# Cached attention of a hybrid decoder step in two sets of four sequences, with the value pages behind the delta rule

## The reference, cut to what matters

```python
kmean = mean of each 256-key block                 # 4 blocks, 8 heads, 8 sequences
gate  = q . kmean ; keep the 3 best past blocks    # per head and sequence
s = q . k * hd ** -0.5 over the kept blocks and the own key
p = softmax(s) ; o = p @ v                         # float32
```

## Time and profile before

| | us |
|---|---|
| median of three runs | 596.73 (593.17 to 600.68) |
| the profiled execution's own time | 596.88 |
| its span | 594.9 |
| TensorE busy | 534.4 (90%) |
| VectorE busy | 350.0 (59%) |
| ScalarE busy | 163.5 (27%) |
| mean granted clock of TensorE | 0.947 |

### The profile page before, as it was taken

One profiled execution on the slowest core, in us unless ns is written; L12 is line 12 of the kernel. 1 busy time (PEld: TensorE's weight loads), 2 busy tenths in 40 slices (PEclk: granted clock), 3 DMA queues, 4 the chain that ended last, 5 costly groups with the idle time before them and its releaser, 6 DMA issues.

```text
span 594.9 us, 10233 instructions
## 1 busy us (share of the span) xinstructions
PE 534.4 (90%) x3943; PEld 450.2 (76%) x3943; DVE 350.0 (59%) x548; ACT 163.5 (27%) x230; POOL 56.6 (10%) x126
## 2 busy tenths in 40 slices
PE   7879997997998888988789689987999999999997
PEld 5557775675688766865564059887999999999996
DVE  4540269478798787955734537465665566455441
ACT  4101010811132122211000224364343443424420
POOL 6800010000104800000101000000000000000000
PEclk8979897997699999999969899998999999999999
DMA  9996356476049467643739998595465655645201
GB/s 294 332 302 207 108 189 218 123 204 221 19 150 324 144 221 245 217 132 119 244 111 376 384 352 268 173 298 163 148 209 162 195 169 168 195 144 193 73 19 37
DMA packets 98998, 116.79 MB, mean 196 GB/s; under 512 B 6317, under 2 KB 81278, under 8 KB 98934
## 3 DMA queue, kind: packets, MB, share of 16 engines
q1 hardware_dynamic: 93218, 104.42, 54.8%
q10 hardware_dynamic: 3908, 7.42, 3.5%
q0 software_dynamic: 1824, 4.30, 2.6%
HBM read 113.30 MB, written 2.99 MB: 195 GB/s over the span
## 4 chain that ended last, share of the span: by engine, by line
PE 64%; DVE 21%; DMA 7%; ACT 3%; issue 3%; ACTq 1%; SPq 0%; DVEq 0%
PE bank L336 61%; DVE prod L916 5%; DVE s_all L1019 5%; DVE mats L916 3%; DMA ring<-in_ada_w_dram 2%; DMA ring<-in_w_out_dram 2%; DVE BTP L916 1%; DVE cv L1127 1%; DMA ring<-in_cache_v_dram 1%; DMA x_nat<-in_x_sample_dram 1%; PE bank L373 1%; PE bank L382 1%; ACT w_part L1692 1%; DMA qb<-q_rows_dram 1%; PE bank L517 1%
## 5 line engine op out<-in xcount | busy, mean ns | idle before, releaser
L336 PE MATMUL bank<-a_hi,w_part 128*128 128x264 f32 x832 | 153.5, 286 | 2.1 <-DVE a_lo L1464 2.1
L916 DVE TENSOR_TENSOR w_part<-ring,w_part 128x2048 fp32r<-128x2048 f32 (+1 forms) x38 | 84.9, 2236 | 89.2 <-ACT w_part L1692 89.2
L336 PEld LDWEIGHTS bank<-a_hi,w_part 128*128 128x128 f32 x832 | 129.8, 189 | 2.6 <-issue 2.6
L336 PE MATMUL bank<-a_lo,w_part 128*128 128x264 f32 x416 | 118.4, 285 | 0.0
L1692 ACT ACTIVATE w_part<-ring 128x2048 fp32r<-128x2048 f32 (+1 forms) x38 | 70.9, 1871 | 86.0 <-PE bank L336 75.0
L336 PE MATMUL bank<-hT,ring 128*128 128x264 f32 x352 | 85.7, 406 | 0.8 <-ACT proj L1555 0.8
L336 PEld LDWEIGHTS bank<-hT,ring 128*128 128x128 f32 x352 | 70.0, 201 | 14.9 <-issue 2.4
L336 PEld LDWEIGHTS bank<-a_lo,w_part 128*128 128x128 f32 x416 | 79.0, 190 | 0.1
L336 PE MATMUL bank<-hid_hi,w_part 128*128 128x264 f32 x352 | 64.9, 285 | 0.0
L336 PEld LDWEIGHTS bank<-ident 128*128 128x128 f32 x362 | 48.1, 212 | 10.4 <-issue 5.6
L336 PEld LDWEIGHTS bank<-hid_hi,w_part 128*128 128x128 f32 x352 | 54.5, 188 | 0.1
(11 more groups left out here) (326 smaller groups left out, 570.3 us busy)
## 6 DMA issues: line engine op xcount, KB each, us to landing
ring<-in_ada_w_dram SPq DMA_DIRECT2D x24, 1024.0 KB, 7.3
ring<-in_cache_k_dram SPq DMA_DIRECT2D x64, 256.0 KB, 3.6
ring<-in_w_in_dram SPq DMA_DIRECT2D x11, 1024.0 KB, 5.6
ring<-in_w_gate_dram SPq DMA_DIRECT2D x11, 1024.0 KB, 5.3
ring<-in_w_up_dram SPq DMA_DIRECT2D x11, 1024.0 KB, 5.3
ring<-in_cache_v_dram SPq DMA_DIRECT2D x40, 256.0 KB, 4.2
ring<-in_w_down_dram SPq DMA_DIRECT2D x8, 1024.0 KB, 5.1
ring<-in_cache_v_dram ACTq DMA_DIRECT2D x24, 256.0 KB, 5.2
```

Source lines behind the costliest of these rows:

```text
L336: return pe.matmul(out, lhsT, rhs, start=start, stop=stop, skip_group_check=True)
L916: return v.tensor_tensor(out, a, b_, op)
```

## The change

The eight sequences are split into two sets of four (`GS`, `GW`). Each set has its own block sums (`G0`, `G1`), maxima, denominators, probabilities and fold (`FO0`, `FO1`), at half the width. Set 0's chain stands between the heads of the prompt attention, and its pages follow the delta rule's end (`V0` to `V3`); the last key item, `K15`, and set 1's `G1` stand among them. `DMAX1` and `DEXP1` follow, with `A9` and `XA` between, then `V4` to `V7` between `XB` and `XD`. `OWN` keeps only the own key's score and moves to before `L1`.

A set's pages now add up in one bank: each sequence has its own 8 of 32 stationary columns, and there is no masking or folding per sequence. At a set's end ScalarE copies the bank (`pv_rows`) and eight matmuls with `selq` select each head's columns and turn them at once. Set 0's probabilities lie in the upper half of `prod`, so the key items of sequences 4 to 7 use the lower half, in four instructions of 1024 columns (`k_item_low`). GpSimd clears the two halves in turn, and stores the tails ahead of the pooling. All pages are issued by SP. `K0` comes after `W8`, and the idle matmuls ahead of the heads' turns are distributed anew. (`QB` tokens have no part on any engine; they are dropped.) The last operations of `OWN` in the old list are the first of `G`.

```diff
+    GS = NS // 2
+    GW = GS * NPG * H
...
-    ORDER = ("W1 W2 QSUM W7 QNORM QR QB0 QB1 K0 W8 K1 K2 W9 CEXT W10 CONV BA AB W3 DSUM QB2 K3 W4 DNORM KSUM K4 GN W5 "
-             "QB3 K5 GC KNORM GBC KR ROWS KK W6 K6 QB4 TI VR L1 K7 KROW W0 K8 M1 VROW L2 QB5 K9 M2 TAILS L3 S K10 M3 A4 "
-             "H0 QB6 K11 L4 M4 H1 A5 H2 L5 K12 M5 A6 QB7 H3 K13 H4 L6 K14 M6 POOL H5 UA A7 K15 H6 UB UC H7 UD A8 HE OWN "
-             "A9 DMAX DEXP V0 XA V1 XB V2 XC V3 XD V4 MX V5 V6 MW0 V7 VE MD MW1").split()
+    ORDER = ("W1 W2 QSUM W7 QNORM QR W8 K0 K1 W9 K2 CEXT W10 CONV BA AB W3 DSUM K3 W4 DNORM KSUM K4 GN W5 "
+             "K5 GC KNORM GBC KR ROWS KK W6 K6 TI VR OWN L1 K7 KROW W0 K8 M1 VROW L2 K9 M2 TAILS L3 S K10 M3 A4 H0 L4 "
+             "H1 M4 A5 K11 H2 L5 M5 H3 G0 A6 H4 L6 DMAX0 K12 M6 POOL H5 DEXP0 UA K13 H6 UB A7 UC H7 K14 UD A8 V0 HE K15 "
+             "V1 G1 V2 V3 FO0 DMAX1 A9 XA DEXP1 V4 XB V5 XC V6 XD MX MW0 V7 FO1 MD MW1").split()
...
-        selc = tmp("selc", [P, NS, 32])
-        dm8 = tmp("dm8", [P, H])
+        selq = tmp("selq", [P, H, GS])
...
-        cmp4 = prod[:, 1024:1024 + NS * NB * H].rearrange("p (q n h) -> p q n h", q=NS, n=NB)
-        pP = prod[:, :].rearrange("p (a m) -> p a m", m=32)
+        pP = [prod[:, o:o + 1024].rearrange("p (a m) -> p a m", m=32) for o in (1024, 0)]
...
+        cmp4 = [w_b[:, o:o + GS * NB * H].rearrange("p (q n h) -> p q n h", q=GS, n=NB) for o in (GW, 0)]
...
-                for _ in range((14, 8, 2, 16, 4, 4, 18, 6)[h]):
+                for _ in range((14, 4, 14, 4, 6, 6, 10, 10)[h]):
...
             def own_scores():
-                keep_awake(6, 8)
                 pe.wait_ge(sem("own_diag"), 1)
-                b = opened("own", 6)
+                b = opened("own", 3)
...
+            def group_sums(g):
+                if g:
+                    keep_awake(6, 8)
+                pe.wait_ge(sem("k_scored"), GS * (g + 1))
+                b = opened(f"gsT{g}", (3, 6)[g])
+                mm(b[:, 0:GW], ones[:, :], s_all[:, g * GW:(g + 1) * GW])
+                for n in range(2):
+                    o = g * GW + n * P
+                    last = pe.transpose(b[:, GW + n * P:GW + (n + 1) * P], s_all[:, o:o + P], ident[:, :])
+                closed(last, f"gsT{g}")
...
+            def spread_max(g):
+                    keep_awake(5, 9)
+                pe.wait_ge(sem("max_diag"), g + 1)
+                b = opened(f"pmax{g}", (3, 5)[g])
+                closed(mm(b[:, 0:GW], ones[:, :], w_a[:, g * GW:(g + 1) * GW]), f"pmax{g}")
...
+            def denominators(g):
+                    keep_awake(5, 5)
+                pe.wait_ge(sem("exps"), g + 1)
+                b = opened(f"den{g}", (3, 6)[g])
+                closed(mm(b[:, 0:GW], ones[:, :], w_b[:, g * GW:(g + 1) * GW]), f"den{g}")
...
             def page_values(q):
-                if q == 0:
-                    keep_awake(4, 9)
-                    pe.wait_ge(sem("p_ready"), 1)
-                b = opened(f"pv{q}", 4 + q % 2)
+                g, j = q // GS, q % GS
+                if j == 0:
+                    if g:
+                        keep_awake(4, 6)
+                    pe.wait_ge(sem("p_ready"), g + 1)
+                    opened(f"pv{g}", (3, 4)[g])
+                b = bank[(3, 4)[g]]
                 for hf in range(HALVES):
                     slot = arrived(pe, ("v", (q, hf))).rearrange("p (k n) -> p k n", k=PGI)
                     for k in range(PGI):
-                        last = mm(b[32 * k:32 * k + 32, :], pP[:, q * NPG + hf * PGI + k, :], slot[:, k, :],
-                                  hf == 0, hf == HALVES - 1)
-                    if hf < HALVES - 1:
+                        last = mm(b[32 * k:32 * k + 32, :], pP[g][:, j * NPG + hf * PGI + k, :], slot[:, k, :],
+                                  j + hf == 0, j == GS - 1 and hf == HALVES - 1)
+                    if j < GS - 1 or hf < HALVES - 1:
                         used_up(last, ("v", (q, hf)), "pe_read")
-                closed(last, f"pv{q}")
-                read_by(f"pv{q}", ("v", (q, HALVES - 1)))
-                if q:
-                    fold(q - 1)
-            def page_end():
-                keep_awake(4, 8)
-                closed(fold(NS - 1), "y8")
-                keep_awake(5, 4)
-                pe.wait_ge(sem("y8_out"), 1)
-                b = opened("yT8", 7)
+                if j == GS - 1:
+                    closed(last, f"pv{g}")
+                    read_by(f"pv{g}", ("v", (q, HALVES - 1)))
+            def fold(g):
+                if g:
+                    keep_awake(5, 6)
+                pe.wait_ge(sem("pv_rows"), g + 1)
+                b = opened(f"yT{g}", (3, 7)[g])
                 for c in range(AC):
-                    last = pe.transpose(b[:, c * P:(c + 1) * P], w_a[:, c * P:(c + 1) * P], ident[:, :])
-                closed(last, "yT8")
+                    for h2 in range(2):
+                        r = 64 * h2
+                        last = mm(b[r:r + 64, c * GS:(c + 1) * GS], stg[:, g, c * P + r:c * P + r + 64], selq[:, 2 * c + h2, :])
+                closed(last, f"yT{g}")
...
+            def k_item_low(q, hf):
+                item = ("k", (q, hf))
+                slot = arrived(v, item)
+                v.wait_ge(sem(f"qb{q % 2}"), 16 * (q // 2 + 1))
+                half = PGI // 2
+                for w in range(2):
+                    ins = tt(prod[:, 0:1024].rearrange("p (k n) -> p k n", k=half),
+                             slot[:, 1024 * w:1024 * w + 1024].rearrange("p (k n) -> p k n", k=half),
+                             bc(qb[:, q % 2:q % 2 + 1, :], [P, half, AW]), ALU.mult)
+                    if w:
+                        used_up(ins, item, "keys_read")
+                        v.wait_ge(*released[item])
+                    else:
+                        step(ins)
+                    o = (q * NPG + hf * PGI + w * half) * H
+                    ins = v.tensor_reduce(s_all[:, o:o + half * H], prod[:, 0:1024].rearrange("p (g d) -> p g d", d=HD),
+                                          AX, ALU.add)
+                    if w and hf == HALVES - 1:
+                        ins.then_inc(sem("k_scored"), 1)
+                        v.wait_ge(sem("k_scored"), q + 1)
+                    else:
+                        step(ins)
...
+            def group_gates(g):
+                v.wait_ge(sem("tails_out"), 64)
+                gate, cnt, cmp = of(gate4, g), of(cnt4, g), cmp4[g]
+                b = full(v, f"gsT{g}")
+                v.tensor_reduce(flat(gate4, g), b[:, 0:GW].rearrange("p (n t h) -> p n h t", t=PPB, h=H), AX, ALU.add)
+                freed(v.tensor_reduce(tokmax[:, 2 * g:2 * g + 2], b[:, GW:2 * GW].rearrange("p (n t) -> p n t", n=2), AX, ALU.max),
+                      f"gsT{g}")
+                v.wait_ge(bank_free[filled[f"gsT{g}"][0]], frees_at(f"gsT{g}"))
+                for n in range(2):
+                    o = g * GW + n * P
+                    last = v.tensor_scalar(w_a[:, o:o + P], ident[:, :], tokmax[:, 2 * g + n:2 * g + n + 1], None, ALU.mult)
+                inc(last, "max_diag")
+                step(v.memset(cnt, 0.0))
                 for m in range(NB):
                     for n0, n1, op in ((0, m + 1, ALU.is_gt), (m + 1, NB, ALU.is_ge)):
                         if n0 < n1:
...
+                            last = tt(cmp[:, :, n0:n1, :], bc(gate[:, :, m:m + 1, :], [P, GS, n1 - n0, H]),
+                                      gate[:, :, n0:n1, :], op)
                     step(last)
...
+                    step(tt(cnt, cnt, cmp, ALU.add))
+                step(v.tensor_scalar(flat(gate4, g), flat(cnt4, g), float(min(TOPK, NB + 1)), None, ALU.is_lt))
+                step(v.tensor_scalar(flat(cnt4, g), flat(gate4, g), FAR, -FAR, ALU.mult, ALU.add))
+            def spread_max(g):
+                e = w_b[:, g * GW:(g + 1) * GW]
+                sm0, sm1, sm2, sm3 = (sm64[:, n, g * GS:(g + 1) * GS, :] for n in range(4))
+                b = full(v, f"pmax{g}")
+                freed(tt(paged(e), paged(b[:, 0:GW]), bc(flat(cnt4, g).unsqueeze(2), [P, GS * NB, PPB, H]), ALU.add), f"pmax{g}")
+                v.wait_ge(bank_free[filled[f"pmax{g}"][0]], frees_at(f"pmax{g}"))
+                step(v.tensor_reduce(sm0, queried(e).rearrange("p q n h -> p q h n"), AX, ALU.max))
+                step(tt(sm1, sm0, sm2, ALU.max))
+                tt(sm3, sm2, sm1, ALU.subtract)
+                step(tt(queried(e), queried(s_all[:, g * GW:(g + 1) * GW]), bc(sm1.unsqueeze(2), [P, GS, NPG, H]), ALU.subtract))
+                inc(v.tensor_scalar(e, e, 0.0, None, ALU.min), "shifted")
+            def denominators(g):
+                e = w_b[:, g * GW:(g + 1) * GW]
+                sm3, sm4, sm5 = (sm64[:, n, g * GS:(g + 1) * GS, :] for n in range(3, 6))
+                v.wait_ge(sem("exp8"), g + 1)
+                inc(tt(paged(e), paged(e), bc(flat(gate4, g).unsqueeze(2), [P, GS * NB, PPB, H]), ALU.mult), "exps")
```

(53 more changed lines are left out.)

137 lines of the change are left out of this document (23 added, 114 removed).

## The result

The changed kernel takes 628.4 us (median of 4 runs, 626.2 to 630.1) against 598.3 us (593.2 to 600.7): ratio 1.050 with the interval 1.045 to 1.055. It is slower, by 30 us; the forecast of 596 us and its whole range of 583 to 608 missed it. The first output-projection matmul starts at 386.04 us where it had started at 356.07; from there to the end of the span the kernel takes 240.4 us against 238.8. So all but 1.5 us of the loss lies where the forecast had looked, between 181 us and the projection.

The account below looks back on a forecast made before the run. VectorE sets the pace, then softmax and DMA-fed page tails run in series. Added work gave +9.0 us at M6 and +2.0 to A8; overlapping the tails put the projection at 355.3 against 356.1: -0.8, 596.1 us, range 583 to 608.

Parts of the forecast that it names:

- The step that failed: Page loads: dropping ScalarE's half costs nothing, as SP issues four pages in 1.9 us against a 2.8 us transfer.
- The landing of V3: Set 0's last pages: with the DMA working through from about 291 us, they land at 308.5 and are used up at 309.5.
- the rival of the absorbed waits: Before A8: VectorE's idle time absorbs the added 18 us; 588 us, or 585 if the second chain hides too; chance 0.3.
- The waits before V0: VectorE's sequence up to M6: added steps and uncovered waits, less moved score items, sum to +9.0 us.
- between M6 and V0: VectorE's stretch with DEXP0, moved key items and extra idle matmuls: +2.0 us up to A8, V0 starting at 293.8.
- low score items: Key items of sequences 4 to 7 in half the buffer: 5.05 instead of 4.65 us each, +0.4.
- The lower-clock rival: TensorE between the sets, 294 to 341 us: a lower clock adds 8 to 10 us, 605 us in all; chance 0.2.
- The chances: Whole kernel: forecast 0.45, absorbed waits 0.3 (a third under 585), lower clock 0.2, rest 0.05; under 585 us given 0.2.
- The second half: From V0 to the projection: DMAX1's product waits behind V3, V4 starts at 328.0 on probabilities, projection at 355.3; the delta step is last.
- the fold, which it put on a branch that is no longer last: End of the page work: the old fold, copy, transposes and reductions are gone, but off the last chain, so no gain counted.

Follow-up runs that it names:

- e1: Changed kernel, but ScalarE issues the second two pages of each value item from sequence 1 on; 619.6 us, ratio 1.033.
- e2: Changed kernel, but SyncE reads the page numbers of V0 to V3 into registers early, still issuing all pages; 616.1 us, ratio 1.027.
- e3: Kernel before the change, but SyncE issues all value pages, ScalarE's halves included; 613.5 us, ratio 1.025.
- e13: Changed kernel's sets and fold in the old order up to OWN, set 0's chain just ahead of V0, set 1's among V0 to V3; 601.1 us, ratio 1.007.
- e6: As e2, with G1, DMAX1 and DEXP1 moved ahead of V1, V2 and V3; 615.1 us, ratio 1.029.
- e9: Changed kernel with early number reads, ScalarE halves of V4 to V7, OWN later, set 1's chain and delta step earlier; 614.8 us, ratio 1.027.
- e12: Changed kernel with score items and A9 ahead of V0, set 0's chain among heads and levels, set 1's under V0 to V3; 616.4 us, ratio 1.030.
- e17: As e13, but G1 ahead of V0, FO0 and XD ahead of V4, fewer idle matmuls, ScalarE's V5 halves before XD; 597.7 us, ratio 0.999.
- e15: As e13, but G1 ahead of V0, FO0 and XD ahead of V4, fewer idle matmuls, eight items' page numbers read early; 609.1 us, ratio 1.013.
- e5: As e2, plus more idle matmuls ahead of TensorE's waits from the first heads to FO0; 629.3 us, ratio 1.051.

## Why the prediction was wrong, point by point

*The step that failed* is the one that costed an edit at nothing: "SP issues four pages in 1.9 us, under the 2.8 the transfer takes, and loses 0.9 per item if it did not". The issues alone take 2.1 us, close to that. What was left out is that each page's number is first read on the same engine, another 2.15 us, so an item takes 4.3 us. The profile of the kernel before had it: the same three small instructions on SyncE's queue, 104 times, in none of the rows that I had drawn on. Here it is in a view of the kernel before:

```profile
L251 SPq TENSOR_LOAD <-table x104: 260/267/558, 34.8 to 331.5; - x104
```

The forecast moved ScalarE's half of this work onto SyncE, looked only at what ScalarE gained, and missed a new bound. e1, e2 and e3 put it at 9 to 13 us. It was not the only step that failed: with it undone, e2 still takes 616.1 us, 8 over the end of the range. The rest is in the next three points.

*The landing of V3* (308.5) was also wrong without this. It let the DMA work through from 291 us. SyncE's timeline in e2, where it is not the limit (first issue, time to the last one, what, issues), shows the order of the issues instead:

```profile
287.41 3.98 SPq L262 DMA_DIRECT2D ring<-in_cache_v_dram  x8
295.47 3.21 SPq L262 DMA_DIRECT2D ring<-in_cache_k_dram  x4
298.86 13.44 SPq L262 DMA_DIRECT2D ring<-in_cache_v_dram  x24
```

V1 is issued at 298.9, behind K15, which waits until 295.5; V3 is used up at 322.6, 21.8 us behind V0, where the forecast had 15.7 and the kernel after has 29.4. So of the 13.7 us that this stretch slipped, SyncE's reads are 7.6 and the order of the issues, with what waits in it, 6.1. The forecast also did not add up what lies between V0 and V7, against what lay there before: 18 MB against 14. Its one total of the kind, fifteen megabytes from V0 in the rival of the absorbed waits, is 3 to 4 short of the 18 to 19 of the windows; and the 585 us of that rival count them from a V0 at 294, where the rival itself has it 8 us earlier.

*The waits before V0* were mostly right in place and too small in sum. VectorE's timeline:

```profile
186.70 0.69 DVE L914 TENSOR_TENSOR BTP<-mats,lvl 128x512 f32<-128x512 f32 x1 [2.68 <-PE bank L336]
...
222.46 0.69 DVE L914 TENSOR_TENSOR BTP<-mats,lvl 128x512 f32<-128x512 f32 x1 [1.89 <-PE bank L336]
...
240.69 0.69 DVE L914 TENSOR_TENSOR BTP<-mats,lvl 128x512 f32<-128x512 f32 x1 [3.83 <-PE bank L336]
...
248.71 0.42 DVE L1357 TENSOR_REDUCE gate<-bank 128x128 f32<-128x256 f32 x1 [1.04 <-PE bank L724]
...
258.85 0.42 DVE L914 TENSOR_TENSOR w_ab<-bank,cnt 128x256 f32<-128x256 f32 x1 [1.99 <-PE bank L336]
```

M1 starts 5.4 us later than before and not 3.0; M4 stands 7.3 us behind H0 (7.0 forecast); M5 waits 3.8 us (2.6); G0's sums 1.0 (1.0); DMAX0 2.0 (2.1). At M6 VectorE is 13.9 us later than before (265.98 against 252.11), where the forecast had 9.0; that is half of the 10.2 us by which V0 was missed. The other half falls between M6 and V0, for which the forecast had 2.0 us. About half of it is the wait for the sums of DEXP0, which made this step 6.1 us long instead of 3.6:

```profile
277.58 0.42 DVE L1396 TENSOR_REDUCE sm<-bank 128x32 f32<-128x256 f32 x1 [3.93 <-PE bank L336]
```

TensorE's clock is 0.73 from 265 to 284 us, where the earlier trace rows has 1.00; how much of the wait that is was not separated. The chain of the kernel after has the low score items close to their forecast cost, four instructions of 1.23 to 1.24 us:

```profile
280.32 1.24 DVE prod L914
281.58 1.23 DVE s_all L1042
282.83 1.24 DVE prod L914
284.09 1.23 DVE s_all L1042
```

The time per item went from 4.65 to 5.02 us (280.32 to the next instruction at 285.35). The rows had given 5.05, the estimate by the Trainium skill (VectorE: DVE Perf Modes, "The TRN2 errata") 4.95. The measured step lies between them, and the trace agrees with the page's fixed time as well: each split of an instruction added 0.17 us, where the estimate has 0.16.

*The lower-clock rival* named the right thing with the right condition: the clock is 0.73, 0.66 and 0.78 behind 304 us, under the 0.85 that it asked for, and XA took 4.48 us instead of 3.27. The trace agrees with the Trainium skill (TensorE: Matmul & The Clock Gate, "HAM oscillation"): waits for the DMA between bursts of matmuls, and the lower clock in them. But it was priced alone at 605 us and had no part in the other cases, and the waits for pages are not all of it: with the pages at full rate (e2, share 1.01) the clock in 304 to 334 us is still 0.77, and in the kernel after it is already 0.73 from 265 to 284 us, ahead of the pages. The rival of the absorbed waits (0.3) is refuted. A DMA queue's own engine as the bound had no chance at all, and none of the cases had two of these losses at once, so the range ended at 608. The chances do not add up either: a third of the 0.3 and all of the rest make 0.15 under 585 us, and the text gives 0.2.

*The second half* was right in kind for the second set: DMAX1 stood behind V3 and FO0, and V4 waited for the probabilities and not for pages. It was wrong for the fold, which it put on a branch that is no longer last. In the last chain of the kernel after, the reciprocal is followed by ScalarE's high part and weight split, then its copy of the page sums (379.38 us), then FO1 and the idle matmuls behind it, up to P at 386.04:

```profile
379.96 1.02 PE L336 MATMUL bank<-selq,stg 128*64 128x4 f32 x16 [3.18 <-ACTq L1590]
380.92 5.37 PE L336 MATMUL bank<-ident 128*128 128x128 f32 x24
```

The same 24 idle matmul instructions ahead of P took 2.84 us in the kernel before; no wait stands between them and P in either. V4 started 18.5 us after V3 was used up in the forecast and 21.9 us in the profile, and the projection 27.3 us after V4 in the forecast and 30.8 in the profile.

The account of the 30 us, then: 9 to 13 page issue on SyncE (shown, by undoing it and by putting it on the old kernel); some 15 the difference between e2 and e13, which is the order (keys and A9 behind the first chain, that chain's steps and OWN among heads and levels) together with the split score items, the idle matmuls and ScalarE's halves. That this bundle carries the 15 us is shown; which part of it does is not: e6 to e9 gave 1 or 2 us each, and e12 is no clean test of the chain. The remaining few are FO0, the roots and page halves in ScalarE's order (e13 against e17, ratios 1.007 and 0.999, with intervals that just part). How the clock shares in these is open.

## What to carry to other kernels

Cost what an issuing engine does for each transfer, and not only the transfer: here reading four page numbers and issuing four pages took 4.3 us for a transfer of 2.8, and moving half of it off ScalarE cost 9 to 13 us on an engine that the busy shares never show. When reads or issues are moved to a wait, look in the trace whether the wait is still there: in e2 it was, in e15 it was only 8 of 18 us long, and the pages came 10 us late. Where two tails are to be laid over each other, add up the bytes that pass behind the start of the second one, before and after: in e2 V0 came 6 us earlier than in the kernel before, with the ring full of other blocks, and the last page 17 us later. And when a single move gives nothing in an in-order kernel, read what stands between the freed step and its user on the consuming engine's queue before trying the next.

## What the runs showed of the hardware

A read of one number from SBUF into a register of SyncE takes 0.27 us, with 0.15 us and gaps behind it 0.54 us per page, and one issue of 256 KB with an address from a register 0.52 us; so in this kernel one queue's engine did not keep the 16 DMA engines busy with 256 KB transfers whose addresses it looked up just ahead of each item (share 0.81, 304 to 334 us); two engines did (1.04 with 369 GB/s in e1), and so did one with the numbers read before (1.01 with 359 GB/s in e2).

Raising the granted clock with idle matmuls was not free: in e5 it went from 0.77 to 1.00 in 304 to 334 us, against e2, and V0, which comes ahead of most of them, was 4.9 us later, the first projection matmul 12.5 us.
